# Absorbing the sample queries between the passes of the cached-key expansion

## The reference

```python
def mla_expand(c_kv, w_kv_b, k_norm):            # 16 heads, 64 + 64 columns each
    kvb = (c_kv @ w_kv_b).reshape(b, S, MLA_HEADS, QK_NOPE + V_HEAD)
    k_nope = rmsnorm(kvb[..., :QK_NOPE], k_norm)
    return k_nope, kvb[..., QK_NOPE:]

def attend(q_nope, q_rope, k_nope, k_rope, v, q_pos, k_pos):
    s = (q_nope . k_nope + q_rope . k_rope) * ATTN_SCALE
    p = softmax(where(mask, s, -inf))
    return p . v
```

## Time and profile before

| | |
|---|---|
| median of 3 runs | 1838.68 us (1837.64 to 1839.15) |
| the profiled execution | 1838.27 us, its span 1836.5 us |
| PE, DVE, ACT busy | 98%, 62%, 45% of the span |
| PE's granted clock | 1.00 throughout |
| passes 0 to 7 | about 1275 to 1388 us of the span |

### The profile page before, as it was taken

The page is one execution under the profiler, slowest core; times in us unless marked ns, Lnnn a source line. Parts: engine busy times, 40 slices in busy tenths (PEclk is TensorE's granted clock), DMA queues, the critical chain, the costliest instruction groups (busy, mean ns, idle before and its releaser), DMA issues.

```text
span 1836.5 us, 28276 instructions
## 1 busy us (share of the span) xinstructions
PE 1807.6 (98%) x10567; PEld 1732.0 (94%) x10567; DVE 1135.9 (62%) x1706; ACT 828.1 (45%) x1420; POOL 228.6 (12%) x280
## 2 busy tenths in 40 slices
PE   9999999999999999999999999999998999999998
PEld 9999999799888999999999999996777999999998
DVE  6454447879889645444775454456778856454445
ACT  6333336665564433333553333346665544333333
POOL 1000110311311000011400001122112131000110
PEclk9999999999999999999999999999999999999999
DMA  6434444456352544454344444451124534444442
GB/s 212 137 116 135 138 138 154 151 207 235 122 206 87 193 125 127 125 150 137 116 142 120 134 117 139 139 171 40 47 82 138 173 116 128 133 121 130 143 138 76
DMA packets 68452, 249.48 MB, mean 136 GB/s; under 512 B 8264, under 2 KB 10568, under 8 KB 67088
## 3 DMA queue, kind: packets, MB, share of 16 engines
q1 hardware_dynamic: 58880, 206.86, 37.1%
q0 software_dynamic: 9488, 41.48, 6.6%
HBM read 235.51 MB, written 12.12 MB: 135 GB/s over the span
## 4 chain that ended last, share of the span: by engine, by line
PE 85%; DVE 9%; ACT 3%; issue 2%; DMA 1%; POOL 0%; DVEq 0%; ACTq 0%; POOLq 0%
PE pair L1913 24%; PE pair L1914 24%; PE pair L1915 24%; DVE wlo L1245 2%; PE pair L2422 2%; PE pair L2331 2%; PE pair L2333 2%; PE pair L2332 2%; DVE cy L1372 1%; DVE S L1468 1%; PE pair L1920 0%; PE pair L1922 0%; PE pair L1921 0%; PE pair L2121 0%; DVE xsT L1475 0%
## 5 line engine op out<-in xcount | busy, mean ns | idle before, releaser
L1913 PE MATMUL pair<-xh,whi 128*128 128x384 f32 x1960 | 660.2, 337 | 2.4 <-DVE xl L1255 1.5
L1915 PE MATMUL pair<-xh,wlo 128*128 128x384 f32 x1960 | 654.9, 334 | 0.0
L1914 PE MATMUL pair<-xl,whi 128*128 128x384 f32 x1960 | 654.8, 334 | 0.0
L1245 DVE TENSOR_TENSOR wlo<-raw,whi 128x1024 fp32r<-128x1024 f32 (+3 forms) x371 | 464.2, 1253 | 160.2 <-ACT whi L708 159.4
L708 ACT ACTIVATE whi<-raw 128x1024 fp32r<-128x1024 f32 (+2 forms) x369 | 378.1, 1028 | 261.7 <-PE pair L1915 257.7
L1913 PEld LDWEIGHTS pair<-xh,whi 128*128 128x128 f32 x1960 | 367.9, 188 | 9.3 <-DVE wlo L1245 3.8
L1914 PEld LDWEIGHTS pair<-xl,whi 128*128 128x128 f32 x1960 | 368.0, 188 | 1.6 <-issue 1.0
L1915 PEld LDWEIGHTS pair<-xh,wlo 128*128 128x128 f32 x1960 | 367.9, 188 | 0.0
L1265 DVE TENSOR_TENSOR tg<-pair,rstd 128x384 f32<-128x384 f32 x88 | 49.1, 557 | 326.1 <-PE pair L1915 325.4
L1913 PE MATMUL pair<-ah,whi 128*128 128x384 f32 x704 | 235.2, 334 | 0.0
L1914 PE MATMUL pair<-al,whi 128*128 128x384 f32 x704 | 235.1, 334 | 0.0
(11 more groups left out here) (408 smaller groups left out, 2198.3 us busy)
## 6 DMA issues: line engine op xcount, KB each, us to landing
raw<-in_stream SPq DMA_DIRECT2D x372, 512.0 KB, 3.7
S<-in_ssm POOLq DMA_DIRECT2D x4, 2048.0 KB, 9.1
out_ssm_s<-S POOLq DMA_DIRECT2D x4, 2048.0 KB, 7.8
seg<-acs_rows POOLq DMA_DIRECT2D x12, 512.0 KB, 5.9
cTb<-in_cacheT POOLq DMA_DIRECT2D x10, 512.0 KB, 4.2
kn<-rs_rows SPq DMA_DIRECT2D x16, 264.0 KB
lowC<-in_cache SPq DMA_DIRECT2D x8, 512.0 KB, 3.2
lowA<-in_cacheT POOLq DMA_DIRECT2D x6, 512.0 KB, 5.1
```

The costliest lines, as they stand in the source:

```text
L1245: V.tensor_tensor(wlo[:, r, 0:w], raw[:, r, 0:w], whi[:, r, 0:w].bitcast(F32), ALU.subtract).then_inc(lo_ready, 1)
L1913: M(out, whi[:, r, ws], mh_(k), start=first and k == k0, stop=False)
L1914: M(out, whi[:, r, ws], ml_(k), start=False, stop=False)
L1915: ins = M(out, wlo[:, r, ws], mh_(k), start=False, stop=last and k == k1 - 1)
```

## The change

The absorption moves into the loop: `absorb(y - 1)` follows expansion 8y + 1 on PE from pass 1 on, and ACT's and DVE's parts follow square and sum 8y + 1; `absorb(7)` and the transpose of the roots follow expansion 58 in pass 7. It writes banks 3, 7 and 5 in place of four others. The weights `wkT` are asked for in passes 0, 2, 4 and 6, each quarter once the prompt scores that used its place are done. `s_scores(0)` stands in pass 7 before expansions 62 and 63, and what it needs moves with it: the three reciprocals of `ksq` (one to the end of pass 6), the square root of `ksq[0:6]` (on ACT before square 53 in place of after square 55), `rope_split(0)`, `keys_split(0)`, and `keys_split(1)` with `rope_split(1)` before square 60 on ACT and before sum 60 on DVE. POOL's order is now rotary rows of 0, latent rows of 0, rotary rows of 1, latent rows of 1, stores of the roots. Stream 1's rows come through `craw` into a buffer of their own, `early`. `s_max(0)` stands before sum 62, `s_max(1)` after sum 63 and before `s_norm(0)`. ACT loads the exponential's table after the last square root, right before `s_exp(0)`. Squares from w = 24 on are written to `sqB`.

```diff
             lowA = sb("lowA", [P, 4096], F32, mla)
-            lowB = sb("lowB", [P, 4096], F32, mla)
+            with ExitStack() as split:
+                lowB = sb("lowB", [P, 4096], F32, split)
+            early = sb("early", [P, 4096], F32R, mla)
             lowC = sb("lowC", [P, 2048], F32, mla)
             Qs = sb("Qs", [P, STREAMS, MH, STEPS], F32, mla)
...
         PTs = lowA[:, 0:2560].rearrange("p (s k q) -> p s k q", s=2, k=5)
+        sqB = lowA[:, 0:1024].rearrange("p (s c) -> p s c", s=2)
+        keys1 = early[:, 0:4 * KEYS].rearrange("p (a k t) -> p a k t", a=2, k=2)
...
         def k_stack(b):
+            if b < 2:
+                return early[0:3 * ROPE, (4 + b) * KEYS:(5 + b) * KEYS]
             return wkh[0:3 * ROPE, b % 2, 0:KEYS]
+
+        def keys_hi(b):
+            return keys1[:, 0] if b == 1 else cTh[:, b % 2]
+
+        def keys_lo(b):
+            return keys1[:, 1] if b == 1 else cTl[:, b % 2]
+
+        def squared(w):
+            return kn[:, w % 2, 0:512] if w < 8 * 3 else sqB[:, w % 2, :]
...
-        QC_BANK = (0, 1, 6, 7)
+        QC_BANK = (3, 7, 3, 7, 3, 7, 3, 5)
...
-            sp.wait_ge(past_sum, 8 * STREAMS)
+            sp.wait_ge(past_sum, 8 * 3)
...
                 pool.dma_start(cTb[:, b % 2, :, 0:PAST], T["cacheT"][b]).then_inc(c_ld[b % 2], 16)
+                if b % 2:
+                    x = MH // 4 * (b // 2)
+                    pool.wait_ge(qk_ps, x + MH // 4)
+                    pool.dma_start(wkT[0:QD, x:x + MH // 4], T["wkT"][:, x:x + MH // 4]).then_inc(wkT_ld, 16)
...
                             pool.dma_start(x[ROPE * r:ROPE * r + ROPE, :, SEQ:TOK], x[NOPE:QD, :, SEQ:TOK]).then_inc(rope_ld, 16)
-            for x in range(0, MH, MH // 4):
-                pool.wait_ge(qk_ps, x + MH // 4)
-                pool.dma_start(wkT[0:QD, x:x + MH // 4], T["wkT"][:, x:x + MH // 4]).then_inc(wkT_ld, 16)
...
             def past_keys(b):
-                if b < 2:
-                    pool.wait_ge(past_ps, 8 * (STREAMS - 1 + b))
+                if b == 0:
+                    pool.wait_ge(past_ps, 8 * (STREAMS - 1))
                     pool.dma_start(cTb[:, b, :, 0:PAST], T["cacheT"][b]).then_inc(c_ld[b], 16)
                 else:
-                    pool.wait_ge(qc_ps, 8)
-                    pool.wait_ge(past_lo, STREAMS + b)
+                    if b == 1:
+                        pool.wait_ge(qc_ps, 7)
+                    else:
+                        pool.wait_ge(past_lo, STREAMS + b)
                     pool.dma_start(craw, T["cacheT"][b]).then_inc(c_ld[b % 2], 16)
...
+            past_rope(0)
             past_keys(0)
-            past_rope(0)
+            past_rope(1)
+            past_keys(1)
             pool.wait_ge(rs_ev, 2)
             pool.dma_start(rs_past(0, 6, 0, 3 * P), rsT[0:6 * MH, :]).then_inc(rs_st, 16)
             pool.dma_start(rs_past(0, 6, 3 * P, P), rsT2[0:6 * MH, 0:P]).then_inc(rs_st, 16)
-            past_keys(1)
             pool.wait_ge(p_masked, MH)
             pool.memset(vnew, 0.0).then_inc(filled, 1)
-            past_rope(1)
             for b in range(2, STREAMS):
                 past_keys(b)
...
                     act.wait_ge(sc_ps, 2 * b - 2)
-                A(cTh[:, s, :, 0:PAST], craw if b >= 2 else cTb[:, s, :, 0:PAST], ACT.Copy)
-                A(cTh[:, s, :, PAST:KEYS], cT[:, :, SEQ + STEPS * b:SEQ + STEPS * b + STEPS], ACT.Copy).then_inc(past_hi, 1)
+                A(keys_hi(b)[:, :, 0:PAST], craw if b else cTb[:, s, :, 0:PAST], ACT.Copy)
+                A(keys_hi(b)[:, :, PAST:KEYS], cT[:, :, SEQ + STEPS * b:SEQ + STEPS * b + STEPS], ACT.Copy).then_inc(past_hi, 1)
+
+            def absorb_hi(j):
+                act.wait_ge(qc_ps, j + 1)
+                for k in range(2):
+                    ins = A(QCh[:, k, :, 2 * j:2 * j + 2, :],
+                            bank[QC_BANK[j]][:, tiles(k, 2 * P)].rearrange("p (h b q) -> p b h q", h=2, b=STREAMS), ACT.Copy)
+                ins.then_inc(qc_hi, 1)
+
...
             for y in range(MH // 2):
+                last = y == MH // 2 - 1
                 for i in range(3):
                     past_square(8 * y + i)
+                    if y and i == 1:
+                        absorb_hi(y - 1)
+                if last:
+                    act.wait_ge(rs_turn_ps, 2)
+                    A(rsT[0:6 * MH, :], bank[4][0:6 * MH, 0:3 * P], ACT.Copy)
+                    A(rsT2[0:6 * MH, 0:P], bank[4][0:6 * MH, 3 * P:4 * P], ACT.Copy).then_inc(rs_ev, 1)
+                    absorb_hi(y)
+                    keys_split(0)
                 p_turned(2 * y)
                 p_turned(2 * y + 1)
                 if y == 0:
                     A(rsT2[0:MH, P:2 * P], bank[2][0:MH, 384:512], ACT.Copy).then_inc(rs_ev, 1)
                 past_square(8 * y + 3)
-                if y + 1 < MH // 2:
+                if last:
+                    keys_split(1)
+                    rope_split(1)
+                else:
                     p_exp(2 * y + 2)
                 past_square(8 * y + 4)
-                if y + 1 < MH // 2:
+                if not last:
                     p_exp(2 * y + 3)
-                else:
-                    keys_split(0)
-                    act.wait_ge(rs_turn_ps, 2)
-                    A(rsT[0:6 * MH, :], bank[2][0:6 * MH, 0:3 * P], ACT.Copy)
-                    A(rsT2[0:6 * MH, 0:P], bank[2][0:6 * MH, 3 * P:4 * P], ACT.Copy).then_inc(rs_ev, 1)
+                if y == MH // 2 - 2:
+                    act.wait_ge(past_sum, 48)
+                    A(ksq[:, :, 0:6], ksq[:, :, 0:6], ACT.Sqrt, bias=EPS, scale=1.0 / NOPE).then_inc(past_std, 1)
                 past_square(8 * y + 5)
...
                     past_split(y + 1)
                 past_square(8 * y + 6)
+                if y == MH // 2 - 2:
+                    rope_split(0)
...
                 if y == MH // 2 - 2:
-                    act.wait_ge(past_sum, 48)
-                    A(ksq[:, :, 0:6], ksq[:, :, 0:6], ACT.Sqrt, bias=EPS, scale=1.0 / NOPE).then_inc(past_std, 1)
-
-
...
             act.wait_ge(past_sum, 8 * STREAMS)
             A(ksq[:, :, 6:8], ksq[:, :, 6:8], ACT.Sqrt, bias=EPS, scale=1.0 / NOPE).then_inc(past_std, 1)
-            rope_split(0)
-            for j in range(8):
-                act.wait_ge(qc_ps, j + 1)
-                for k in range(2):
-                    ins = A(QCh[:, k, :, 2 * j:2 * j + 2, :],
-                            bank[QC_BANK[j % 4]][:, tiles(k, 2 * P)].rearrange("p (h b q) -> p b h q", h=2, b=STREAMS), ACT.Copy)
-                ins.then_inc(qc_hi, 1)
-                if j == 5:
-                    act.preload_act_table(ACT.Exp)
...
+            act.preload_act_table(ACT.Exp)
+            s_exp(0)
...
-            s_exp(0)
-            keys_split(1)
-            rope_split(1)
...
                 for i in range(8):
                     past_sums(8 * y + i)
-                    if i == 4 and not more:
-                        keys_split(0)
+                    if y and i == 1:
+                        absorbed(y - 1)
                     if i == 2 and more:
...
-                    if not more and i < 3:
+                    if y == MH // 2 - 2 and i == 7:
                         dve.wait_ge(past_std, 1)
-                        V.reciprocal(ksq[:, :, 2 * i:2 * i + 2], ksq[:, :, 2 * i:2 * i + 2]).then_inc(past_rstd, 1)
...
-
-            for j in range(6):
-                absorbed(j)
...
-
-            s_max(0)
-            absorbed(6)
-            absorbed(7)
+                        V.reciprocal(ksq[:, :, 0:2], ksq[:, :, 0:2]).then_inc(past_rstd, 1)
+                    if not more:
+                        if i == 2:
+                            rope_split(0)
+                        if i < 2:
+                            V.reciprocal(ksq[:, :, 2 * i + 2:2 * i + 4], ksq[:, :, 2 * i + 2:2 * i + 4]).then_inc(past_rstd, 1)
+                        if i == 2:
+                            absorbed(y)
+                            keys_split(0)
+                        if i == 3:
+                            keys_split(1)
+                            rope_split(1)
+                        if i == 5:
+                            s_max(0)
+
+            s_max(1)
             for u in range(UNITS):
-                s, o = u % 2, 64 + 8 * (u % 2)
-                dve.wait_ge(s_exp_ready, u + 1)
-                step(V.reciprocal(sm[:, o + 5:o + 6], sm[:, o + 4:o + 5]))
-                V.tensor_scalar(Pb[:, s, 0:KEYS], Pb[:, s, 0:KEYS], sm[:, o + 5:o + 6], None, ALU.mult).then_inc(p_ready, 1)
-                if u == 0:
-                    keys_split(1)
-                    rope_split(1)
-                elif u % 2 == 0 and u // 2 + 1 < STREAMS:
+                s_norm(u)
+                if u and u % 2 == 0 and u // 2 + 1 < STREAMS:
                     rope_split(u // 2 + 1)
...
+            def absorb(j):
+                pe.wait_ge(wkT_ld, 16 * (j // 2 + 1))
+                if j < MH // 2 - 1:
```

(52 more changed lines are left out.)

124 lines of the change are left out of this document (56 added, 68 removed).

## The result

The changed kernel took 1842.87 us (median of 11 runs, 1842.19 to 1845.1), the kernel before beside it 1839.25 us (11 runs, 1837.64 to 1840.99): ratio 1.0023, 95% interval 1.0015 to 1.003. So it is slower: by the ratio 0.23%, by the two medians 3.6 us, which is 0.20%. The forecast was 1842.5 us, +3.8 on the median. The profiled execution took 1843.06 us with a span of 1841.2.

A forecast was written before the change was run, and what follows sets the result against it. PE, busy 98% of the span, bounds the kernel; DVE bounds pass 7. 5.6 + 1405.1 - 1406.65 = +4.05 us, by PE's pauses +4.3; +4.2 on the profiled 1838.27 gives 1842.5 us, range 1838.5 to 1846.0.

The forecast's parts named there:

- Passes 1 to 6: In the loop: one absorption per pass, PE without free time, each costing 0.93 us, 5.6 us later at pass 6's end.
- growth by less than 0.9 us: Sign in the loop's passes: if they grow by less than 0.9 us, the prediction is wrong.
- The root before square 53: End of pass 6: table load and root on ACT delay square 53 and so expansion 56 by 1.82 us.
- Steps 1 to 5: Pass 7 to unit 0's transposes: DVE's order and stream 1's rows make PE wait, 3.6 us before the transposes at 1402.5.
- the landing: Pass 7: stream 1's latent rows, issued at 1385.7, land 4.87 us later at 1390.6; uncertainty -0.8 to +0.9 us.
- Step 6: First units: transposes (0.55) and `s_scores(2)` (1.95), so `s_max(2)` starts at 1405.1 on the old clock.
- rival C: Behind PE's 3.6 us pause: more waits than counted; a halved clock adds +3 us (1845.5), late roots +2; chance 0.12.
- the forecast's line of 0.2%: Whole kernel: 0.2% (3.7 us, 1842.4) is about what a measurement can tell from no change; forecast just above.
- Rival A: After pass 6: DVE keeps ahead in pass 7 and 5.7 us of pauses go, 1832.6 us; chance 0.07.
- Rival B: Little changes: the root is free, or rows land early and sums overlap more, 1840.7 down to 1838.7 us; chance 0.23.
- The +2 us that I kept for late roots: Before `s_max(0)`: SP's load of the roots, issued about 1389, must land by 1395.5; counted as nothing, +2 us kept.

The follow-up runs named there:

- the run with the rotary rows first: Changed kernel with DVE's `rope_split(0)` before sum 57 in place of after the third reciprocal: 1841.64 us, ratio 1.0014.
- the early table: Changed kernel with root back, rotary rows split earlier, exponential before last root, and the exponential's table loaded in pass 7 before the roots' transpose: 1837.58 us, ratio 0.9993.
- pieces-alone kernel: Kernel before with only the absorptions moved into the passes, with their banks and the loads of `wkT`: 1845.75 us, ratio 1.0035.
- The version with all three: Changed kernel with root back behind square 55, `rope_split(0)` before sum 57, and `s_exp(0)` before the last root, `s_norm(0)` before `s_max(1)`: 1838.63 us, ratio 1.000.
- the changed kernel with filling and later value rows: Changed kernel with twelve unread products before unit 0's transposes, and stream 1's value rows requested after the roots' rows of units 2 and 3: 1841.93 us, ratio 1.0018.

## Why the prediction was right

The prediction was right in sign, size and in most of its steps, and partly by luck: two errors of about a microsecond cancelled. It set `s_max(2)` at +4.05 us against the kernel before; the trace shows 1410.87 - 1406.65 = +4.22.

**Passes 1 to 6: 5.6 us said, 5.1 found.** ACT's first `p_turned` row of each pass gives the lengths. From pass 0 to pass 6 these rows run from 1281.72 to 1372.06 in the changed kernel and from 1281.57 to 1366.78 in the one before: 5.28 us in all, of which 0.15 was there at the first. 5.13 us for six pieces is 0.86 each; five passes grew by 0.88 to 0.92, and one by 0.64, the one that took 14.50 us in the kernel before, where the others took 14.11 to 14.24. The prediction named growth by less than 0.9 us as a sign that it is wrong. Taken by the letter that sign is there, with a mean of 0.86; the bound stood too close to its own 0.93, since each pass still took a whole absorption without a pause. Doubling the pieces cost 0.87 each again. DVE and ACT were covered, the early `wkT` loads never late.

**The root before square 53: 1.82 said, 1.84 found** (1381.70 - 1374.58 - 5.28), and 1.75 came back when it was moved. The Trainium skill (ScalarE: Activation LUTs, What ACT_TABLE_LOAD costs) puts a drain of about 1.38 us on top of the load's 1.283. No run here shows it: load, root and square 53 stand end to end at 1376.50, 1377.79 and 1378.22, and taking the root away gave 1.75 to 1.92 us, not the 3.2 that load, drain and root would make. The measurement decides.

**Steps 1 to 5: 0.8 us too late.** Seen from expansion 56 the forecast put `rope_split(0)`'s end at 7.8 us (found 7.55), the issue of the `craw` rows at 9.3 (9.07), their arrival at 14.2 (13.43), `s_max(0)` at 19.1 (18.25), the transposes at 26.1 (25.30). Most of it is one term: the landing took 4.36 us, not the chain's 4.87. The order of waits was as said: the third reciprocal before `rs_turn` (1.00 for 1.2), ACT at `keys_split(1)`, square 60 (0.28 for 0.7), `s_max(0)` (1.03 for 1.4) and the long pause released by `s_norm(0)` (3.58 for 3.6). That POOL's release is what holds `s_max(0)` the run with the rotary rows first has shown: DVE's one instruction earlier, and `s_max(0)` 1.86 us sooner.

**Step 6: 1.3 us too early.** Transposes and `s_scores(2)` were costed at 2.6 us; from the transposes' start to `s_max(2)` it took 3.87, and 2.61 where the pause was filled and the row moved, at a clock of 1.00. So the 1.26 us between are the clock. That is rival C's mechanism: behind the pause the clock was halved. I had given it 0.12 as an alternative to the forecast, at +3 us. It happened inside the forecast, at +1.3, since the slow stretch was 3.4 us long (1407.7 to 1411.1) and little over a us was lost in it before `s_max(2)`. So C was right in the place and in kind, and its price 2.4 times too high. The rule of the Trainium skill (TensorE: Matmul & The Clock Gate, What's actually happening), that full speed is granted only after recent activity, agrees with this trace (0.50 behind a pause of 3.58 us); it should have raised C's chance.

The sum of the terms: -0.32 (passes, with the drift of 0.15) + 0.02 (root) - 0.8 (steps 1 to 5) + 1.27 (clock) = +0.17, which is 4.22 - 4.05. Behind `s_max(2)` the distance was not quite kept: POOL's request for stream 4's rows came 3.67 us later than before, and that for stream 6's 4.46, behind an `s_max(8)` that had waited 0.69 us for its row of roots; the profiled execution ended at +4.79. The forecast by medians, +3.8, met +3.6. The ratio (0.23%) lies just above the forecast's line of 0.2% and the difference of the medians (3.6 us) just under it, so the run does not tell which side of the line is right.

**Rival A** (the tail closes) fails where the forecast said, on DVE and the landing, yet it isn't out of reach: three small moves take the change's cost away, and with the early table the median lies 1.5 us under that of the kernel before, where A promised 5.7. **Rival B** would nearly have been right had the root been free: without it the median is 1841.07, where B ended at 1840.7. The +2 us that I kept for late roots did not occur, but the margin was small. In the changed kernel's chain that ended last (start, us, what) the roots' store and row follow each other:

```profile
1391.84 3.83 DMA rs_rows<-sqt
1395.68 3.43 DMA kn<-rs_rows
```

By this chain the row is there at 1399.11, 0.84 us before `s_max(0)` uses it. In the pieces-alone kernel, where the roots' rows are asked for only after the last sum, `s_max(0)` waits 3.83 us for one.

**What the change is worth in the end.** Moving the absorptions costs PE the same work and takes away its cover: alone +6.5 us. The rest wins back 2.9. The three waits that it introduced itself are worth 4.2, and the kernel with them undone and the table early is at 0.9993 (0.9984 to 1.0002) of the kernel before: not told apart from it by these runs. Whether it wins anything stays open. The row of roots for unit 2 held `s_max(2)` in two traces, 1.02 us by the profile's own reading and 0.87 by the comparison of two traces; moving half a MB from ahead of it changed no median beyond its interval.

## What to carry to other kernels

Work moved from behind a loop into a full loop is not saved, it only loses its second use as cover; ask first what it was hiding, since that is what will be seen next. When one engine's order is written by hand, price each moved instruction by who stands behind it: one root and one table load ahead of a square cost 1.8 us, a table load at an idle place of the same engine nothing. A pause that a few instructions have made longer (here `s_max(1)` and a table load ahead of `s_norm(0)`) can be long enough for the clock to fall, so look at the granted clock in the stretch behind each pause, not only at the pause.

## What the runs showed of the hardware

The clock. It fell to 0.50 at pauses of 3.10, 3.37, 3.55, 3.57 and 3.58 us, in each of the five kernels that had one that long: in four of them while PE still stood, in the changed kernel 0.7 us after it had taken up work. With the pause filled or shortened to 0.94 us or less it stayed at 1.00 there. Between these lengths it went either way. The kernel before kept 1.00 through pauses of 2.10 and 1.74 us. The version with all three lost it some 2 us after one of 2.06 (at 1404.5, with another wait of 0.51 between), and the pieces alone lost it a second time 1.2 us after one of 1.92. Of five kernels with 1.68 to 1.70 us before `rs_turn` four kept it, and one, with 1.70, lost it 1.4 us later. The slow stretches lasted 3.4 us in five places, 6.8 in two and 10.2 in one. So a pause of some 2 us is a risk. It may also make executions of one kernel differ; with one trace of each kernel that is not shown.

A late row of roots. In the steady units POOL asks for a stream's rows every 9.04 us. In seven of the thirteen traces one of these distances was 0.7 to 2.2 us longer. In all seven DVE's `s_max(8)` had just waited for its row of roots (264 KB), 0.65 to 2.13 us, and in none of the other six. In the changed kernel:

```profile
1439.49 0.71 DVE L1841 TENSOR_TENSOR Pb<-pair,kn 128x528 f32<-128x528 f32 x1 [0.69 <-DMA kn<-rs_rows]
```

This row was asked for at 1432.52, 6.97 us before; in the kernel before `s_max(8)` started 6.21 us after the request without a wait. ACT waits for a stream's rows in the steady units of every trace, also of those that keep the 9.04, so that wait alone does not make a distance longer; in one of the seven, the changed kernel with filling and later value rows, it may have added about 0.5 us. From `s_max(2)` to the end of the span it is 429.5 to 430.3 us in the six traces without a late row and 430.1 to 432.8 in the seven with one, the longest three being those where `s_max(12)` had to wait as well. Why the row is late in some executions no run here shows. The traces also drift apart before the loop (by 1.3 us among most; one lay 5 us late), and so single traces are compared here only stretch by stretch.
